# Fourier mix from even and odd parts of the positions, and column sums of squares partly added on VectorE, in a float32 two-block transformer kernel

## What is computed

```
h = rmsnorm(h_res) ; u, c, b, v, gates = split(h @ w_in)       # u: (272, 4 groups x 128)
y_a = real(fft2(u per group, over positions and channels)) @ w_fourier
y_b = (b * conv3(c * v)) @ w_conv_out
mix = (sig(gate0) * y_a + sig(gate1) * y_b) @ w_out
h_res = h_res + rmsnorm(mix) ; h2 = rmsnorm(h_res)
up = conv3(h2 @ w_up) ; h_res += rmsnorm((gelu(a) * v) @ w_down)
```

## Time and profile before

| | us |
|---|---|
| median of 3 runs | 1016.21 |
| the three runs | 1016.21, 1016.39, 1013.99 |
| the profiled execution's own time | 1014.2 |
| its span, first to last instruction | 1012.4 |
| TensorE busy in it | 988.0 |
| VectorE busy | 587.2 |
| ScalarE busy | 531.0 |
| GpSimd busy | 351.6 |
| mean granted TensorE clock | 0.995 |

### The profile page before, as it was taken

The page is one execution under the profiler, slowest core; times in us unless marked ns, Lnnn a source line. Parts: engine busy times, 40 slices in busy tenths (PEclk is TensorE's granted clock), DMA queues, the critical chain, the costliest instruction groups (busy, mean ns, idle before and its releaser), DMA issues.

```text
span 1012.4 us, 15035 instructions
## 1 busy us (share of the span) xinstructions
PE 988.0 (98%) x6334; PEld 891.7 (88%) x6334; DVE 587.2 (58%) x787; ACT 531.0 (52%) x717; POOL 351.6 (35%) x108
## 2 busy tenths in 40 slices
PE   7999999999999998999999999999999899999997
PEld 6888889999888887789999888899899899999885
DVE  4997946888222545446887222444117479888643
ACT  6676346554333666646555333645444577566432
POOL 0021045656666545255655665455430000000000
PEclk9999999999999999999999999999999999999999
DMA  8453234545555443344454654444334425455541
GB/s 334 166 198 130 84 121 159 180 173 202 184 190 207 164 169 124 126 143 157 175 194 167 209 206 175 173 171 172 125 126 166 167 102 208 170 184 192 180 153 41
DMA packets 24787, 168.78 MB, mean 167 GB/s; under 512 B 2784, under 2 KB 3056, under 8 KB 4880
## 3 DMA queue, kind: packets, MB, share of 16 engines
q1 hardware_dynamic: 24432, 167.49, 46.0%
q10 hardware_dynamic: 288, 0.33, 0.1%
HBM read 166.77 MB, written 1.05 MB: 166 GB/s over the span
## 4 chain that ended last, share of the span: by engine, by line
PE 92%; DVE 3%; ACT 3%; issue 1%; DMA 1%; SPq 0%; DVEq 0%; ACTq 0%
PE bank L626 28%; PE bank L628 28%; PE bank L627 28%; PE bank L819 2%; PE bank L1012 1%; ACT whi L1114 1%; PE bank L654 1%; PE bank L1033 1%; DMA h<-x_rows 1%; DVE wlo L1663 1%; PE bank L1000 1%; PE bank L787 0%; PE bank L836 0%; PE bank L912 0%; PE bank L855 0%
## 5 line engine op out<-in xcount | busy, mean ns | idle before, releaser
L2285 POOL TENSOR_TENSOR wlo<-raw,whi 128x1024 fp32r<-128x1024 f32 (+1 forms) x102 | 350.7, 3440 | 398.9 <-ACT whi L1114 391.3
L1663 DVE TENSOR_TENSOR wlo<-raw,whi 128x1024 fp32r<-128x1024 f32 (+2 forms) x152 | 246.8, 1624 | 320.0 <-ACT whi L1114 319.9
L1114 ACT ACTIVATE whi<-raw 128x2048 fp32r<-128x2048 f32 (+1 forms) x154 | 292.8, 1902 | 150.9 <-PE bank L628 149.9
L626 PE MATMUL bank<-nhi,whi 128*128 128x256 f32 (+3 forms) x840 | 241.4, 287 | 4.5 <-DVE nlo L2177 3.2
L627 PE MATMUL bank<-nlo,whi 128*128 128x256 f32 (+3 forms) x840 | 238.8, 284 | 0.0
L628 PE MATMUL bank<-nhi,wlo 128*128 128x256 f32 (+3 forms) x840 | 238.4, 284 | 0.0
L626 PEld LDWEIGHTS bank<-nhi,whi 128*128 128x128 f32 (+1 forms) x840 | 160.7, 191 | 9.2 <-issue 9.1
L627 PEld LDWEIGHTS bank<-nlo,whi 128*128 128x128 f32 (+1 forms) x840 | 160.9, 192 | 0.1
L628 PEld LDWEIGHTS bank<-nhi,wlo 128*128 128x128 f32 (+1 forms) x840 | 161.0, 192 | 0.0
L626 PE MATMUL bank<-mhi,whi 128*128 128x258 f32 x384 | 110.2, 287 | 1.0 <-DVE mlo L2132 1.0
L628 PE MATMUL bank<-mhi,wlo 128*128 128x258 f32 x384 | 108.4, 282 | 0.0
(11 more groups left out here) (272 smaller groups left out, 1556.5 us busy)
## 6 DMA issues: line engine op xcount, KB each, us to landing
raw<-w_stream SPq DMA_DIRECT2D x154, 1024.0 KB, 4.8
cst<-consts SPq DMA_DIRECT2D x1, 1200.0 KB, 11.6
h<-x_rows SPq DMA_DIRECT2D x4, 256.0 KB, 5.1
raw<-w_stream SPq DMA_DIRECT2D x2, 512.0 KB, 6.5
out_rows<-e SPq DMA_DIRECT2D x4, 256.0 KB, 2.0
b<-consts_x SPq DMA_DIRECT2D x1, 544.0 KB, 5.5
e<-g_post SPq DMA_DIRECT2D x1, 512.0 KB, 3.9
raw<-w_stream SPq DMA_DIRECT2D x1, 352.0 KB, 9.4
```

The costliest lines, as they stand in the source:

```text
L626: pe.matmul(out, lhsT.hi, rhs.hi, start=start, stop=False)
L1114: act.activation(whi[j][:, 0:n], raw[j][:, 0:n], ACT.Copy).then_inc(s_hi.up(i))
L1663: dve.tensor_tensor(wlo[j][:, 0:m], raw[j][:, 0:m], whi[j][:, 0:m].bitcast(F32), ALU.subtract).then_inc(s_lod.up(i))
L2285: pool.tensor_tensor(wlo[j][:, m:n], raw[j][:, m:n], whi[j][:, m:n].bitcast(F32), ALU.subtract).then_inc(s_lop.up(i))
```

## The change

1. The transform over the positions uses the symmetry of the 272-point circle. DVE forms e[t] = u[t] + u[272 - t] and o[t] = u[t] - u[272 - t] (a mirrored read of `UT`) into `EO`, eight instructions of 136 or 135 elements and one copy. Cosine rows 0 to 136 then act on e (the row of 136 halved in the constant), sine rows 1 to 135 on o. `dc` becomes four products of 128 columns, with stationary operands of 128, 128, 9 and 7 columns, into one bank; the 9 and the 7 land on partitions 0 and 32 of the third column block. ACT copies the bank in three pieces; the two short ones share `P1r`, 39 partitions of which GpSimd zeroes the gap once. `dp` becomes two products with 128 rows and one with 39.
2. Sum 0: DVE adds up the first seven squares in `SQA`, one 258-column addition per block, between its weight tiles; PE multiplies `SQA` and the last square by the ones.
3. Sum 1: PE adds squares 0 to 3 singly, after `rough` of features 0 and 1 and of 2 and 3; DVE adds 4, 5 to 6, 7 (`SQB`, 516 columns) and PE takes the two results after `rough` of features 4 and 5. Four groups by two (features 6 and 7) follow it, where eight by two (4 to 7) followed the last column sum before.

```diff
@@ tensor_program
-                    on.wait_ge(*use["u", g].gone())
-                    for i, (c, n) in enumerate(((META, P), (META + P, P), (0, META))):
-                        u = begin("dc", g, i)
-                        pe.matmul(u.t[0:n, 0:256], UT[:, g, c:c + n], dftc, start=True, stop=True).then_inc(u.full)
+                    u = begin("dc", g)
+                    on.wait_ge(*s_eo.at(g, 1))
+                    on.wait_ge(*s_eo0.at(0))
+                    for c, n, row, col, j in ((0, P, 0, 0, 0), (HALF + 1, P, 0, P, 1),
+                                              (P, HALF + 1 - P, 0, 2 * P, 0), (HALF + 1 + P, HALF - 1 - P, 32, 2 * P, 1)):
+                        x = pe.matmul(u.t[row:row + n, col:col + P], EO[:, g, c:c + n], dftc[:, j * P:j * P + P], start=True, stop=True)
+                    x.then_inc(u.full)
...
+                    for j in range(2):
+                        pe.matmul(u.t[:, 0:N2], P1[:, j * P:j * P + P], dl[:, j, X0:L2], start=j == 0, stop=False)
+                    pe.matmul(u.t[:, 0:N2], P1r[:, g % 2, :], cm[:, X0:L2], start=False, stop=True).then_inc(u.full)
...
-                for k in ((0, 1) if g == 2 else (g - 1,)):
-                    col_add(0, k)
-            col_add(0, 7)
+            col_sum(0, [(SQA, s_sqa.at(6)), (SQ[:, 1, 0:N2], s_sq.at(7))])
...
-            for j in range(2):
+            for j in range(3):
                 for k, n, av in product((2 * j, 2 * j + 1), range(2), range(2)):
                     rough(n, av, k)
-                for k in (range(2), range(2, 8))[j]:
-                    col_add(1, k)
-            for n, k, av in product(range(2), range(4, 8), range(2)):
+                if j < 2:
+                    col_sum(1, [(SQ8[:, k, :], s_sq8.at(j)) for k in (2 * j, 2 * j + 1)], j == 0, False)
+                else:
+                    col_sum(1, [(SQB[:, i, :], s_sqb.at(0)) for i in range(2)], False)
+            for n, k, av in product(range(2), range(6, 8), range(2)):
                 rough(n, av, k)
@@ vector_program
+            for g in range(4):
+                on.wait_ge(*use["u", g].gone())
+                mirror = UT[:, g, ::-1]
+                dve.tensor_tensor(EO[:, g, 1:HALF + 1], UT[:, g, 1:HALF + 1], mirror[:, 0:HALF], ALU.add).then_inc(s_eo.up(g, 0))
+                dve.tensor_tensor(EO[:, g, HALF + 1:L2], UT[:, g, 1:HALF], mirror[:, 0:HALF - 1], ALU.subtract).then_inc(s_eo.up(g, 1))
...
+            on.wait_ge(*s_sq8.at(3))
+            dve.tensor_tensor(SQB, SQ8[:, 4:6, :], SQ8[:, 6:8, :], ALU.add).then_inc(s_sqb.up(0))
             lo(UP2 + 2)
@@ gpsimd_program
+                if i == IN2 + 2:
+                    for q in range(4):
+                        on.wait_ge(*use["out", 3, q].gone())
+                    pool.memset(P1r, 0.0).then_inc(s_rest.up(0))
```

More of the change, by code:

```diff
@@ L22 @@
 N2 = L2 - X0
+HALF = L2 // 2
+REST = 32 + HALF - 1 - P
 SLOT = 2048
@@ L91, in constants @@
     k = np.outer(np.arange(L2), np.arange(L2)) % L2
-    dl = np.stack([np.cos(2 * np.pi * k / L2), -np.sin(2 * np.pi * k / L2)], 1) * scale
-    dl = dl.astype(np.float32)
-    dlx = np.ascontiguousarray(dl[META:].reshape(2, P, 2, L2).transpose(1, 0, 2, 3).reshape(P, 4 * L2))
+    cos, sin = (f(2 * np.pi * k / L2) * scale for f in (np.cos, np.sin))
+    cos[HALF] *= 0.5
+    dlx = np.stack([cos[0:P], -sin[1:P + 1]], 1).astype(np.float32).reshape(P, 2 * L2)
+    dlm = np.zeros((REST, L2), np.float32)
+    dlm[0:HALF + 1 - P] = cos[P:HALF + 1]
+    dlm[32:REST] = -sin[P + 1:HALF]
     tri_s = (s >= t).astype(np.float32)
-    return c, dlx, np.ascontiguousarray(dl[:META].reshape(META, 2 * L2)), tri_s
+    return c, dlx, dlm, tri_s
 class Pair:
@@ L361, in plan_banks @@
     feat("bg", IN2 + 6, 4, 2)
-    feat("gt", IN2 + 8, 16, 2, lambda g: {0: [("dc", g // 4, i) for i in range(3)], 2: [("dp", g // 4)]}.get(g % 4, ()))
+    feat("gt", IN2 + 8, 16, 2, lambda g: {0: [("dc", g // 4)], 2: [("dp", g // 4)]}.get(g % 4, ()))
     for part in range(2):
@@ L367, in plan_banks @@
                 last[tile] = ((name, m), 0)
-    banks.take("cn", 0, hold=True, signals=8)
+    banks.take("cn", 0, hold=True)
     feat("mo", OUT2, 8, 2)
     banks.drop("cn", 0)
-    banks.take("cn", 1, hold=True, signals=8)
+    banks.take("cn", 1, hold=True)
     for n in range(22):
@@ L549, in block_kernel @@
         YB = A.pair(4 * N2).view("p (k t) -> p k t", k=4)
-        cm = A(2 * L2)[0:META, :]
-        P1s = [A(3 * 256).rearrange("p (t n) -> p t n", t=3) for _ in range(2)]
-        dlx = A(4 * L2)
+        cm = A(L2)[0:REST, :]
+        P1s = [A(256) for _ in range(2)]
+        P1r = A(2 * P)[0:REST, :].rearrange("p (j n) -> p j n", j=2)
+        dlx = A(2 * L2)
+        EOF = A(4 * L2)
+        EO = EOF.rearrange("p (k t) -> p k t", k=4)
         assert A.at <= o_meta
@@ L555, in block_kernel @@
         UN = nT2[:, :, X0:L2]
+        SQA = EOF[:, 0:N2]
+        SQB = EOF[:, N2:3 * N2].rearrange("p (k t) -> p k t", k=2)
         UF, SQ8 = GT[:, 0:8, :], cgcv.rearrange("p (k t) -> p k t", k=8)
-        dl = dlx.rearrange("p (t j l) -> p t j l", t=2, j=2)
-        cmv = cm.rearrange("p (j l) -> p j l", j=2)
+        dl = dlx.rearrange("p (j l) -> p j l", j=2)
         dftc = const("dftc")
@@ L602, in block_kernel @@
         s_cvid, s_ybhi, s_yblo, s_fthi = (sig(n, range(4)) for n in ("cvid", "ybhi", "yblo", "fthi"))
+        s_eo, s_eo0, s_rest = sig("eo", grid(4, 2)), sig("eo0", [0]), sig("rest", [0])
         s_mg, s_mghi, s_mglo = (sig(n, range(8)) for n in ("mg", "mghi", "mglo"))
@@ L605, in block_kernel @@
         s_cv = sig("cv", grid(2, 2))
+        s_sqa, s_sqb = sig("sqa", range(1, 7)), sig("sqb", [0])
         s_fc, s_ge, s_fm, s_ffh, s_ffl = sig("fc", grid(22, 2)), *(sig(n, range(22)) for n in ("ge", "fm", "ffh", "ffl"))
@@ L1005, in dft @@
                     on.wait_ge(*TD)
-                    n = 0
-                    for i in range(3):
-                        on.wait_ge(*use["dc", g, i].gone())
-                        for j in range(2):
[L1010 to L1014, removed]
+                    on.wait_ge(*s_rest.at(0))
+                    on.wait_ge(*use["dc", g].gone())
+                    for j in range(2):
+                        pe.matmul(u.t[:, 0:N2], P1[:, j * P:j * P + P], dl[:, j, X0:L2], start=j == 0, stop=False)
+                    pe.matmul(u.t[:, 0:N2], P1r[:, g % 2, :], cm[:, X0:L2], start=False, stop=True).then_inc(u.full)
             blocks("gt", IN2 + 8, 16, X0, dft)
@@ L1023, in tensor_program, with col_sum @@
                          lambda k: s_yblo.at(k), 4, YB)
[L1025 to L1033, removed]
+            def col_sum(c, parts, first=True, end=True):
+                u = begin("cn", c) if first else use["cn", c]
+                for i, (x, ready) in enumerate(parts):
+                    on.wait_ge(*ready)
+                    y = pe.matmul(u.t[:, 0:N2], ones, x, start=first and i == 0, stop=end and i == len(parts) - 1)
+                if end:
+                    y.then_inc(u.full)
             us = [begin("mo", g) for g in range(2)]
@@ L1063, in tensor_program @@
             weights_in(UP2)
-            begin("cn", 1)
             def rough(n, av, k):
@@ L1526, in dft @@
                     g = g // 4
[L1527 to L1533, removed]
+                    u = use["dc", g]
+                    on.wait_ge(*u.done())
+                    on.wait_ge(*s_rest.at(0))
+                    if g >= 2:
+                        on.wait_ge(*use["dp", g - 2].done())
+                    act.activation(P1s[g % 2], u.t[:, 0:256], ACT.Copy)
+                    act.activation(P1r[0:HALF + 1 - P, g % 2, :], u.t[0:HALF + 1 - P, 2 * P:3 * P], ACT.Copy)
+                    act.activation(P1r[32:REST, g % 2, :], u.t[32:REST, 2 * P:3 * P], ACT.Copy).then_inc(u.free)
                 elif g % 4 == 2:
@@ L1556, in col_rms @@
                 u = use["cn", c]
-                on.wait_ge(*u.done(7))
+                on.wait_ge(*u.done())
                 act.activation(RS[:, 0:N2], u.t[:, 0:N2], ACT.Ln, bias=eps, scale=1.0 / D).then_inc(u.free)
@@ L1567, in scalar_program @@
                 if g >= 2:
-                    on.wait_ge(*use["cn", 0].done(g - 2))
+                    on.wait_ge(*s_sqa.at(max(1, g - 2)))
                 act.activation(SQ[:, g % 2, 0:N2], u.t[:, 0:N2], ACT.Square).then_inc(s_sq.up(g))
@@ L2154, in vector_program @@
             merged_lo(7)
-            for g in range(0, 8, 2):
-                lo(OUT2 + g // 2 + 2)
+            on.wait_ge(*use["dc", 3].done())
+            for g in range(8):
+                if g % 2 == 0:
+                    lo(OUT2 + g // 2 + 2)
+                if 1 <= g < 7:
+                    on.wait_ge(*s_sq.at(g))
+                    if g > 1:
+                        on.wait_ge(*s_sqa.at(g - 1))
+                    dve.tensor_tensor(SQA, SQ[:, 0, 0:N2] if g == 1 else SQA, SQ[:, g % 2, 0:N2], ALU.add).then_inc(s_sqa.up(g))
             on.wait_ge(*s_rs.at(0))
```

2 lines of the change are left out of this document (1 added, 1 removed).

## The result

| | before | after |
|---|---|---|
| median, us | 1015.1 (4 runs) | 1005.17 (4 runs) |
| lowest and highest | 1013.09, 1016.39 | 1003.66, 1006.55 |
| the profiled execution | 1014.2 | 1006.29 |
| its span | 1012.4 | 1004.5 |
| mean granted clock in it | 0.995 | 0.993 |

The ratio is 0.9906 with a 95% interval of 0.9891 to 0.9921: 9.5 us faster, between 8.0 and 11.1. The forecast was 8.3 us less and 1007.9 us; the time lies in the range of 1003.8 to 1011.5.

The account below looks back on a forecast made before the run. TensorE was taken to bound the kernel. Fourier mix -6.2, sum 0 -2.6 and sum 1 +0.5 gave -8.3 us, so 1007.9 us against the median of 1016.21, range 1003.8 to 1011.5.

Parts of the forecast that it names:

- What bounds the kernel: Whole kernel: TensorE, busy 988.0 of 1012.4 us; a removed instruction saves its full distance to the next start.
- Price of a product: Float32 products on TensorE: 0.435 us each for 258 columns, 0.22 for 128 columns.
- dc: First Fourier-mix block: from 1.60 to 1.34 us, a gain of 0.26 per group, bounds 0.10 and 0.41.
- dp: Second Fourier-mix block: from 2.99 to 1.69 us, a gain of 1.30 per group, up to 1.68.
- VectorE's work for `EO`: Additions ahead of the tile at 669.13: about 2.6 us within 4.51 us idle, costing nothing.
- Rival E: Mirrored reads on VectorE so slow that TensorE waits; 1022 us at 3.0 us each; chance 0.03.
- Sum 0: First column sum, behind the last block: eight products become two, saving 2.6 us.
- Sum 1: Column sum within `rough`: ends 2.0 us later, so n = 4 starts 0.5 us later, with 1.4 us new waiting.
- Rival B: Sum 1 pays too, ScalarE or VectorE making up 2 us between 823 and 840; 1006.5 us; chance 0.12.
- rival C: Half-clock stretch after a TensorE wait: one more, 1011.0 us, chance 0.15; one fewer, 1004.8 us, chance 0.08.
- The likeliest case: Whole kernel: the forecast itself, 1007.9 us against the median; chance 0.57.
- The sum: Whole kernel: -6.2 - 2.6 + 0.5 = -8.3 us, taken from the median of 1016.21 us.

Follow-up runs that it names:

- x6: Kernel after with the third dp product on 128 rows instead of 39, the added rows zeros; 1001.19 us in one execution.
- x2: Kernel before with both column sums done as after, Fourier mix as before; 1011.76 us, ratio 0.997.
- x5: Kernel after with the 7-column product moved from PSUM partitions 32 to 38 to partitions 0 to 6; 1004.44 us in one execution.
- x3: Kernel after with sum 1's two products on `SQB` put ahead of the rough products of features 4 and 5; 1003.48 us, ratio 0.9891.
- x4: Kernel after with sum 1 as before, eight products; 1006.48 us in one execution.
- x1: Kernel after with both column sums done as before, so the Fourier part alone; 1006.22 us, ratio 0.9914.
- x7: Kernel after with seven additional unused 258-column products filling TensorE's wait before `rough`; 1002.19 us, ratio 0.9876.
- x8: Kernel after with the changes of x3, x6 and x7 together; 1000.12 us, ratio 0.9858.

## Why the prediction was right, point by point

- **What bounds the kernel.** Right. The removed products came off at their distance from start to start; TensorE stayed at 97%.
- **Price of a product.** Right: x6's three products take 1.30 against 1.31, and the six products that sum 0 saves 2.64 (x2) against 2.61.
- **dc, the mis-sized term.** I took 0.15 us for the step from 9 to 7 columns and let the two run one after the other: 1.34. It is 0.96. The step costs nothing (x5: 1.17, against 4 x 0.22 + 0.31 = 1.19 without it), and the two run at once (x5 against after: 0.21). Four groups: 1.5 us of the gain that I left out. This is the rule of the Trainium skill, "TensorEngine Tiling (Array Packing)", Key Properties, that the prediction set beside the sum: no drain between tiles of one mode, and tiles that run at the same time. The traces agree, 0.96 where it gave about 0.97. I had treated a rule without a row as no evidence; x5 is its row.
- **dp.** Right in size (1.70 against 1.69) and cause: the 39 rows are loaded late on both sides, and with 128 rows the loss is gone (x6).
- **VectorE's work for `EO`.** Nothing waited for it, as said. The usual price of a mirrored addition was right, 0.29 us against 0.30, but not the first one's:

```profile
668.05 2.49 DVE L2107 TENSOR_TENSOR b<-b 128x136 f32<-128x136 f32 x1
670.46 0.29 DVE L2108 TENSOR_TENSOR b<-b 128x135 f32<-128x135 f32 x1
...
672.64 1.23 DVE L1671 TENSOR_TENSOR wlo<-raw,whi 128x1024 fp32r<-128x1024 f32 x1 [0.55 <-ACT whi L1121]
...
666.95 3.44 POOL L2312 TENSOR_TENSOR wlo<-raw,whi 128x1024 fp32r<-128x1024 f32 x1 [2.61 <-ACT whi L1121]
```

  It starts while GpSimd works on its half of the weight tile and ends right after that does (670.54 and 670.39). So the block takes 4.0 us, not 2.6, of the 4.5 that were idle; 0.55 is left, less than I had said. Rival E, a slow mirrored read, falls. The first addition takes 2.49 or 2.50 us in the eight other traces that have it too, and ends right after GpSimd's subtraction each time. That GpSimd holds VectorE up is read from these rows; no run tested it.
- **Sum 0.** Right: 2.6 us (x2: 2.64), and the tail behind the last block is unchanged, 801.88 - 797.31 = 4.57 us as 808.73 - 804.16 before.
- **Sum 1.** Right, the mechanism too: 0.38 to 0.44 us dearer, forecast 0.5; the root 1.98 us later, forecast 2.0; and the wait for the tile of n = 4 where it was said to be. Rival B falls with x2, x3 and x4. The profile puts down 0.70 us to that wait, but the new waiting is 1.4 us in all, as forecast: 1.30 - 0.35 = 0.95 at n = 4, and 0.2 each around the transposes ahead of n = 2 and n = 3 (818.10 - 817.55 = 0.55 us where 0.35 is usual, for one).
- **The clock, rival C.** The likeliest case held at the median, but the mechanism was at work in the profiled execution: one half-clock stretch more, at 403 us and not where I had looked for it, and a shorter one at the start of `rough`. That the four runs of either kernel fall two and two on the two levels, to go by their times, so that the medians can be compared, is luck. What is open: why the stretch at 403 follows the same wait in some executions and not in others (it is in the traces of after, x1, x2 and x4), why it was in none of the eight of x7 and x8, to go by their mean clock, and why the one at the start of `rough` is short (0.76) in all four traces that have one at 403 and long (0.56 to 0.61) in four of the five that have none.
- **The sum.** -7.7 - 2.6 + 0.4 = -9.9 us, against 9.5 by the ratio and 9.9 by the medians; the forecast's -8.3 lacks the 1.5 us of dc. The median of 1007.9 us lies 2.7 too high, 1.6 for the gain and 1.1 because the median of the kernel before is 1015.10 with its fourth run and was 1016.21.

## What to carry to other kernels

Where TensorE is the bound, a saved product is worth its full start-to-start distance, but a reduction moved later in the program can lose more than it saves: ask who waits for its result, and put it as early as its input allows (x3). Keep stationary operands at the full row count where zeros cost nothing (x6), and put small ones side by side in different column places. Before a small gain is judged, sort the executions by granted clock: one stretch at half clock here is worth as much as a quarter of the change.

## What the runs showed of the hardware

- Products with 9 and 7 stationary columns on PSUM partitions 0 and 32 share their time: 0.96 us for the block against 1.17 with both on partition 0.
- A stationary operand of 39 rows between operands of 128 costs 0.40 us (1.70 against 1.30), nearly as much as a whole product of 258 columns (0.435).
- Behind a wait of TensorE of 2.87 us half clock followed in four traces (after, x1, x2, x4) and not in six others with the same wait; behind one of 3.23 us it followed in all nine traces that have that wait, for stretches of unlike length (0.56 to 0.76 as the mean of 7 us). Runs at a mean clock of 0.993 and at 0.995 differ by some 2.5 us. Filling the second wait kept the clock up, but gave only half of what the clock had cost from there to n = 4, since VectorE's low parts were next.
- An addition of 136 elements on VectorE took 2.49 us where it started inside GpSimd's subtraction, and 0.28 or 0.29 in the seven that followed, all of them reading one operand mirrored.
